# A fused two-block network on one core: two modulation groups summed by VectorE behind attention, one moved into routing, and scatter weights turned by transposes

## The chip, the cores and the metric
One core of a Trainium2 chip runs the whole program in one launch. The metric is the device time of one execution in microseconds; lower is better.

## The reference, cut to what matters
The model has 256 tokens of width 1024 and a context of as many rows. The first block is attention (dilated and sliding-window), a norm, and 32 experts of which each token takes 4. The second block has two layers; each begins with a modulation that depends only on two vectors, c (for the tokens, "latent") and c_ctx (for the context):

```python
sc, sc_ctx = jax.nn.silu(c), jax.nn.silu(c_ctx)
for i in range(DEPTH_2):                       # 2 layers
    last = i == DEPTH_2 - 1
    m  = (sc @ w_mod[i] + b_mod[i]).reshape(bsz, 6, d)
    mc = (sc_ctx @ w_mod[i] + b_mod[i]).reshape(6, d)
    sh1, s1, g1, sh2, s2, g2 = [m[:, j, None, :] for j in range(6)]
    sh1c, s1c, g1c, sh2c, s2c, g2c = [mc[j] for j in range(6)]
    h_lat = x * (1.0 + s1) + sh1
    ...
    if not last:
        ctx = layer_norm_2(DN_ALPHA * ctx + g1c * mix_ctx, ...)
```

w_mod is 2 x 1024 x 6144 floats, 48 MB. In the last layer the context's rows are used for shift 1 and scale 1 alone.

## The kernel before, in words
**Weights.** All large weights go through a ring of six slots in SBUF (class Ring, L135). A chunk is 128 x 4096 floats, 2048 KB. `program` (L3633) writes the list of chunks `front`; chunk n takes slot n mod 6. SP issues the loads in that order on one queue, and waits before each until the slot's last chunk has been given back (`chunk_used`). The list: eleven chunks w_in0 to 10, w_mod chunks put between them by the table MODS_BEHIND, w_proj_a, w_proj_b (2), w_out (2), the last four w_mod chunks, then six per expert (moe0.0 to moe31.5), and eight chunks for the context stream among the experts'. From expert 26 on the ring has five slots.

**Modulation** (class Modulation, L271) comes in 6 groups of 2048 columns, each of 4 chunks ("quarters"): groups 0 to 2 are layer 0, groups 3 to 5 layer 1 (3 is shift 1 and scale 1). There are two ways to compute a group. Either VectorE multiplies each half chunk by a column of silu(c) and adds it to a sum of 128 x 2048, one sum for each stream (`add`, L311), so 16 passes a group, and TensorE adds the sum's partitions up with 8 products (`reduce`, L330); or TensorE multiplies the chunks directly (`quarters`, L343), 32 products. Both begin with four products for the biases (`biased`, L295). ACT copies the result out of PSUM (`scalar`), POOL stores it to DRAM (`store`).

**Attention** (function `attention`, L392) has one instruction stream per engine. TensorE makes q, k and v, then 24 units (8 dilated, 16 sliding-window). In a unit TensorE turns the probabilities, makes the scores of the unit after next and then a "piece" of other work that fills the wait for ACT's copy; then the output products. The pieces are the 8 gate tiles in thirds (4, 8 and 4 products) and, before the change, two halves of group 3 (units 4 and 5). Groups 0 to 2 are summed by VectorE before the units. Group 4 is done by TensorE directly behind the units, ahead of the projections. Then TensorE makes eight tiles m0 to m7 of the projections, which VectorE merges with the gates (L830, `merged_ready`), and, after all eight, the four products x0 to x3 with w_out (tile 0 left and right, tile 1 left and right). VectorE adds each to the residual and normalises a tile after its second half.

SP loads up to the chunk behind w_out (`ring.load(sp, ring.at["w_out"] + 3)`, L472), waits for the eighth merge, loads rows, router weights and ctx, goes on with the ring to moe0.1, waits for the norm (`y_ready`), loads the experts' biases, four more chunks, and waits for the biases to land (`loaded`) before it ends its block. All engines end a block together.

**Routing** (class Router, L1285) turns the normed tiles, makes logits, chooses four experts per token, and TensorE has the quarters of group 5 between these steps.

**Experts** (function `moe`, L1410; `expert`). Per expert TensorE makes 4 products for biases, four chunks (16 records each), gathers rows for an expert to come (L1522), turns h with four transposes (L1591), scatters the last expert's result (L1536), turns the scatter weights by two products with the identity (L1598), does a part of the context stream's work where there is one, and two more chunks. A chunk's slot is given back when its products are done. Behind the experts come two stages with gathers of table rows (L1884, L3103) and a linear attention.

## Time and profile before
| | us |
|---|---|
| median of 3 runs | 3541.35 (3540.29 to 3546.61) |
| profiled execution, its own time | 3540.89 |
| its span | 3539.0 |
| PE busy | 3196.0 (90%) |
| DVE busy | 1861.4 (53%) |
| ACT busy | 1112.9 (31%) |
| POOL busy | 877.7 (25%) |
| HBM read | 1366.60 MB, 386 GB/s over the span |

PE is TensorE's products, DVE is VectorE, ACT is ScalarE, POOL GpSimd, SP the engine that issues the loads. Times in the trace count from the span's start. Attention and routing reach 338.7 us, the experts to 1338. A float32 product has two records in PE's counts, a transpose one. The share of an engine over the whole span says little here, since the stages have different limits.

### The profile page before, as it was taken

Reading aid. Unit: us, or ns where it says so; the run is one execution under the profiler, and the core shown is the slowest. Engines: PE = TensorE matmul, PEld = TensorE weight load, DVE = VectorE, ACT = ScalarE, POOL = GpSimd, SP = SyncE. Lnnn points to the kernel's source line nnn. Section 1 sums busy time; section 2 is a strip of 40 time slices with the busy share of each in tenths; the row PEclk is TensorE's granted clock in tenths of the full one; section 3 lists DMA queues with packets and bytes.
Section 4 is the critical chain, followed back from the end, with each engine's and each line's share of the span. In section 5 each row is a group of like instructions: output and inputs, shape, how many; then the busy total and the mean of one; then the engine's idle time right before and its main releaser. Section 6 shows DMA issues by size and latency. Waiting matters only on the chain. (4 is left out here: it accounts for less than half of the span.)

```text
span 3539.0 us, 34401 instructions
## 1 busy us (share of the span) xinstructions
PE 3196.0 (90%) x11192; PEld 1424.6 (40%) x11192; DVE 1861.4 (53%) x4137; ACT 1112.9 (31%) x2999; POOL 877.7 (25%) x796
## 2 busy tenths in 40 slices
PE   8999999999999997989899879998888988877776
PEld 7565343434334433443344323343334444422222
DVE  7743112111221127676776777668764487667664
ACT  1241111110110114444444544445333124434333
POOL 0000000000000003444444444445440024444442
PEclk9999999999999999999999999999999999999999
DMA  9737999999999999999999999999997169999998
GB/s 406 323 144 296 426 427 426 422 419 425 410 428 428 399 427 394 413 421 421 414 416 417 419 421 411 407 421 411 421 403 296 68 278 402 421 421 416 411 419 333
DMA packets 155585, 1370.05 MB, mean 387 GB/s; under 512 B 18335, under 2 KB 18847, under 8 KB 23950
## 3 DMA queue, kind: packets, MB, share of 16 engines
q0 software_dynamic: 111360, 805.46, 55.2%
q1 hardware_dynamic: 44046, 562.36, 38.0%
q8 instruction: 94, 1.54, 0.2%
q14 instruction: 85, 0.70, 0.0%
HBM read 1366.60 MB, written 1.15 MB: 386 GB/s over the span
## 5 line engine op out<-in xcount | busy, mean ns | idle before, releaser
L3103 PE MATMUL ps<-sb_arena,sb_diag 128*128 128x512 f32 x3072 | 1487.6, 623 | 285.6 <-ACT sb_diag L3078 284.5
L1884 POOL DMA_INDIRECT sb_arena<-in_uv,sb_idx x768 | 865.0, 1126 | 2302.1 <-PE ps L3103 1067.2
L3033 DVE SCALAR_TENSOR_TENSOR sb_arena<-sb_arena,sb_H 128x1024 f32<-128x1024 f32 x768 | 941.2, 1226 | 583.6 <-DMA sb_arena<-in_uv,sb_idx 389.0
L3103 PEld LDWEIGHTS ps<-sb_arena,sb_diag 128*128 128x128 f32 x3072 | 562.1, 195 | 1161.4 <-ACT sb_diag L3078 610.1
L1545 PE MATMUL ps<-sb_ring,sb_arena 128*64 128x512 f32 x3072 | 674.4, 594 | 3.6 <-DMA sb_ring<-in_moe 3.6
L3069 ACT ACTIVATE sb_act<-sb_dots 128x1 f32<-128x1 f32 x768 | 154.8, 202 | 1023.3 <-DVE sb_arena L3033 1019.6
L1545 PEld LDWEIGHTS ps<-sb_ring,sb_arena 128*64 128x64 f32 x3072 | 214.3, 137 | 441.7 <-issue 430.0
L1746 DVE TENSOR_SCALAR sb_arena<-ps 128x512 f32<-128x512 f32 x32 | 22.1, 692 | 593.0 <-PE ps L1545 577.4
L3078 ACT ACTIVATE sb_diag<-sb_consts,sb_act 128x128 f32<-128x128 f32 x768 | 308.5, 402 | 28.6 <-PE ps L3103 3.5
L3073 ACT ACTIVATE sb_act<-sb_act,sb_wts 128x1 f32<-128x1 f32 x768 | 226.2, 295 | 25.1
L183 PE MATMUL ps<-sb_ring,sb_arena 128*128 128x512 f32 x416 | 182.0, 594 | 1.9 <-DVE sb_arena L832 1.3
L183 PEld LDWEIGHTS ps<-sb_ring,sb_arena 128*128 128x128 f32 x416 | 77.9, 190 | 97.9 <-issue 96.1
L1753 DVE TENSOR_SCALAR sb_arena<-ps 128x512 f32<-128x512 f32 x32 | 22.1, 692 | 155.1 <-PE ps L1545 155.1
L1662 ACT ACTIVATE sb_arena<-sb_arena 128x512 f32<-128x512 f32 x32 | 20.2, 630 | 249.6 <-DVE sb_arena L1746 249.6
L183 PE MATMUL ps<-sb_ring 128*128 128x128 f32 (+2 forms) x448 | 88.9, 354 | 6.4 <-ACTq L3455 2.9
L388 POOL DMA_DIRECT2D mod_rows<-sb_arena x24 | 12.5, 527 | 329.7 <-ACTq L374 329.7
L1656 ACT ACTIVATE sb_arena<-ps 128x512 f32<-128x512 f32 x32 | 19.1, 597 | 229.3 <-PE ps L1522 229.3
L1679 ACT ACTIVATE sb_arena<-ps 128x512 f32<-128x512 f32 x32 | 19.1, 597 | 227.5 <-PE ps L1545 227.5
L2341 PE MATMUL ps<-sb_ring 128*128 128x512 f32 x192 | 86.4, 593 | 0.0
L183 PEld LDWEIGHTS ps<-sb_ring 128*128 128x128 f32 x448 | 67.9, 194 | 34.8 <-issue 27.5
L183 PE MATMUL ps<-sb_arena,sb_ring 128*128 128x256 f32 x352 | 76.9, 379 | 0.7 <-PE ps L351 0.4
L183 PEld LDWEIGHTS ps<-sb_arena,sb_ring 128*128 128x128 f32 x352 | 66.5, 190 | 10.9 <-issue 2.0
(364 smaller groups left out, 2504.4 us busy)
## 6 DMA issues: line engine op xcount, KB each, us to landing
sb_ring<-in_moe SPq DMA_DIRECT2D x192, 2048.0 KB, 16.4
sb_ring<-in_w_mod SPq DMA_DIRECT2D x24, 2048.0 KB, 14.5
sb_ring<-in_w_in SPq DMA_DIRECT2D x10, 2048.0 KB, 15.7
sb_ring<-in_a_w_in SPq DMA_DIRECT2D x8, 2048.0 KB, 13.6
sb_ring<-in_b_w_in SPq DMA_DIRECT2D x8, 2048.0 KB, 13.0
sb_ring<-in_w_q SPq DMA_DIRECT2D x6, 2048.0 KB, 13.3
sb_arena<-in_uv,sb_idx POOLq DMA_INDIRECT x768, 14.8
sb_ring<-in_a_w_out SPq DMA_DIRECT2D x4, 2048.0 KB, 12.8
```

What stands on the lines that cost most here:

```text
L183: last = nc.tensor.matmul(out, lhs, rhs, start=i == 0, stop=i == len(pairs) - 1)
L1545: last = nc.tensor.matmul(m.ps[n * SLOTS:(n + 1) * SLOTS, bank, :], lhs(k + KT // 2 * (c % 2), n), w[:, k, n * 512:(n + 1) * 512], start=f ...
L1662: nc.scalar.activation(x.sig, x.g, ACT.Sigmoid, scale=SW_ALPHA).then_inc(M(name("sig_ready", p)), 1)
L1746: nc.vector.tensor_scalar(x.g, m.ps[:, 4, :], LIMIT, None, ALU.min).then_inc(M(name("g_ready", p)), 1)
L1753: nc.vector.tensor_scalar(x.u, m.ps[:, 5, :], LIMIT, -LIMIT, ALU.min, ALU.max).then_inc(M(name("u_ready", p)), 1)
L1884: pool.indirect_dma_start(row_buffer(m, n), None, d[f"uv{layer}"], bass.IndirectOffsetOnAxis(m.idx[:, pair % 2, k:k + 1], 0))\
L2341: last = nc.tensor.matmul(m.ps[:, where[0], :], lhs(k), w[:, k, :], start=k == 0, stop=k == KT - 1)
L3033: nc.vector.scalar_tensor_tensor(out=u, in0=u, scalar=1.0, in1=m.H[:, order[i], :], op0=ALU.mult, op1=ALU.mult, accum_out=m.dots[:, n_ % P ...
L3069: nc.scalar.activation(a, m.dots[:, n_ % PK:n_ % PK + 1], ACT.Gelu_apprx_tanh).then_inc(M("gelu_done"), 1)
L3073: nc.scalar.activation(a, a, ACT.Copy, scale=m.wts[:, pair % 2, k:k + 1]).then_inc(M("act_ready"), 1)
L3078: nc.scalar.activation(m.diag[n_ % DIAGS], m.const("ident"), ACT.Copy, scale=a).then_inc(M("diag_ready"), 1)
L3103: last = nc.tensor.matmul(out[h], m.diag[n_ % DIAGS], uv[b][:, D + h * 512:D + (h + 1) * 512], start=opens, stop=ends)
```

## The change
1. Group 3 leaves the pieces of attention: the pieces are the 24 thirds of the gates alone, two ahead of the units, so the last two units have none. Group 3 is now computed by TensorE in routing, where group 5 was, and its chunks are loaded last, ahead of the experts'.
2. Group 4 leaves TensorE. VectorE sums it behind attention, for the latent stream only (8 passes): three quarters ahead of the first merge, the fourth ahead of the merge of m3. TensorE's `reduce` has 4 selecting products instead of 8 and stands behind m7.
3. Group 5 is summed by VectorE likewise: a quarter ahead of the merge of m5, one each ahead of x0, x1 and x2. TensorE's `reduce` of it stands ahead of x3.
4. With one sum, each pass waits for the pass before it; with two sums it waited for the last but one.
5. The table of loads: w_in7 to w_in10 follow w_in6 and its chunks directly, then w_mod16 to 19, w_proj_a, w_proj_b, w_out, w_mod20 to 23, w_mod12 to 15.
6. Per expert, the scatter weights are turned by `nc.tensor.transpose` in place of a product with the identity.

```diff
-LATE_MODS = 1
-SUMMED_MODS = 3
-MOD_FILL, MOD_END = 3, 4
-MODS_BEHIND = (1, 3, 4, 6, 8, 9, 12, 16, 16, 16, 20)
+MOD_ORDER = (0, 1, 2, 4, 5, 3)
+FIRST_MODS = 3
+LATE_MOD = MOD_ORDER[-1]
+MODS_BEHIND = (1, 3, 4, 6, 8, 9, 12)
...
+        self.sums = {0: gates, 1: tokens, 2: gates, 4: [m.part(0, 2048)], 5: [m.part(2048, 2048)]}
...
         for k in range(2):
-            for stream in range(2):
-                out, scale = self.sums[i % 2][stream], self.silu_c[:, 2 * quarter + k, stream:stream + 1]
-                if self.adds >= 2:
-                    dve.wait_ge(M("mod_add"), self.adds - 1)
+            for stream, out in enumerate(self.sums[i]):
+                scale, behind = self.silu_c[:, 2 * quarter + k, stream:stream + 1], len(self.sums[i])
+                if self.adds >= behind:
+                    dve.wait_ge(M("mod_add"), self.adds - behind + 1)
...
         self.biased(pe, i)
-        pe.wait_ge(self.M("mod_summed"), i + 1)
+        pe.wait_ge(self.M("mod_summed"), MOD_ORDER.index(i) + 1)
...
-    pieces = [("gate", n, third) for n in range(8) for third in range(3)]
-    pieces[6:6] = [("mod", MOD_FILL, half) for half in range(2)]
-    ahead = len(pieces) - len(units)
+    pieces = [(n, third) for n in range(8) for third in range(3)]
+    ahead = 2
     gm = banks.plan([("m", i) for i in range(KT)], [0, 1, 2, 3])
+    mod.plan([4, 5], [0, 1])
...
-                piece(*pieces[ahead + u])
+                if ahead + u < len(pieces):
+                    piece(*pieces[ahead + u])
...
-            mod.tensor(pe, MOD_END)
...
+            mod.reduce(pe, 4)
             pe.wait_ge(M("merged_ready"), KT)
             for i in range(4):
+                if i == 3:
+                    mod.reduce(pe, 5)
                 t, half = i // 2, i % 2
...
+            for quarter in range(3):
+                mod.add(dve, 4, quarter)
             for i in range(KT):
                 where = gm["m", i]
+                if i == 3:
+                    mod.add(dve, 4, 3)
+                if i == 5:
+                    mod.add(dve, 5, 0)
...
             for i in range(4):
+                if i < 3:
+                    mod.add(dve, 5, 1 + i)
                 t, half = i // 2, i % 2
...
-                    last = nc.tensor.matmul(m.ps[:, 4, t * P:(t + 1) * P], x.weigh[:, t, :], m.const("ident"), start=True, stop=True)
+                    last = nc.tensor.transpose(m.ps[:, 4, t * P:(t + 1) * P], x.weigh[:, t, :], m.const("ident"))
...
-            end = MODS_BEHIND[n]
-            front += [(f"w_mod{u}", d["w_mod"][u], SLOT) for u in range(sent, end)]
-            sent = end
+            if n < len(MODS_BEHIND):
+                front += [mod_chunk(u) for u in range(sent, MODS_BEHIND[n])]
+                sent = MODS_BEHIND[n]
+        front += [mod_chunk(u) for u in range(16, 20)]
         front += [("w_proj_a", d["w_proj_a"], 2 * D)]
         front += [("w_proj_b", d["w_proj_b"][n], SLOT) for n in range(2)]
         front += [("w_out", d["w_out"][n], SLOT) for n in range(2)]
-        front += [(f"w_mod{u}", d["w_mod"][u], SLOT) for u in range(4 * (N_MOD - LATE_MODS), 4 * N_MOD)]
+        front += [mod_chunk(u) for u in (*range(20, 24), *range(12, 16))]
```

SP's order from the load of ctx to the second chunk of the experts; ctx, the router's weights and the two rows of L907 (L912 now) stand behind SP's wait for the eighth merge, and `chunk_usedN` is the giving back of slot N. Before:

```order
L1297 DMA sb_X<-in_ctx 128x2x1024
L152 DMA sb_ring<-in_w_mod 128x4096 [waits chunk_used1]
L152 DMA sb_ring<-in_w_mod 128x4096 [waits chunk_used2]
L152 DMA sb_ring<-in_w_mod 128x4096 [waits chunk_used3]
L152 DMA sb_ring<-in_moe 128x4096 [waits chunk_used4]
L152 DMA sb_ring<-in_moe 128x4096 [waits chunk_used5]
```

And now:

```order
L1302 DMA sb_X<-in_ctx 128x2x1024
L152 DMA sb_ring<-in_w_mod 128x4096 [waits chunk_used3]
L152 DMA sb_ring<-in_w_mod 128x4096 [waits chunk_used4]
L152 DMA sb_ring<-in_w_mod 128x4096 [waits chunk_used5]
L152 DMA sb_ring<-in_w_mod 128x4096 [waits chunk_used0]
L152 DMA sb_ring<-in_w_mod 128x4096 [waits chunk_used1]
L152 DMA sb_ring<-in_w_mod 128x4096 [waits chunk_used2]
L152 DMA sb_ring<-in_w_mod 128x4096 [waits chunk_used3]
L152 DMA sb_ring<-in_moe 128x4096 [waits chunk_used4]
L152 DMA sb_ring<-in_moe 128x4096 [waits chunk_used5]
```

Four w_mod chunks more (w_mod12 to 15) stand between the wait for the merges and the experts' first chunk.

TensorE's order from x1 to the first turned tile (L183 are w_out's products, L1316 and L1321 the transposes of y). Before:

```order
L183 MATMUL ps<-sb_ring,sb_arena 128x512 [waits bank_free5,chunk_in5]
L183 MATMUL ps<-sb_ring,sb_arena 128x512 x7
L183 MATMUL ps<-sb_ring,sb_arena 128x512 [waits bank_free6,chunk_in4]
L183 MATMUL ps<-sb_ring,sb_arena 128x512 x7
L183 MATMUL ps<-sb_ring,sb_arena 128x512 [waits bank_full6,bank_free7,chunk_in5]
L183 MATMUL ps<-sb_ring,sb_arena 128x512 x7
L1316 MATMUL ps<-sb_consts,sb_X 128x128 [waits bank_full7,y_ready,bank_free4]
L1316 MATMUL ps<-sb_consts,sb_X 128x128 x3
L1316 MATMUL ps<-sb_consts,sb_X 128x128 [waits y_ready,bank_free5]
```

And now, from x1 on, where L304 are the bias products and L342 the selecting products of group 5:

```order
L183 MATMUL ps<-sb_ring,sb_arena 128x512 [waits bank_free5,chunk_in1]
L183 MATMUL ps<-sb_ring,sb_arena 128x512 x7
L183 MATMUL ps<-sb_ring,sb_arena 128x512 [waits bank_free6,chunk_in0]
L183 MATMUL ps<-sb_ring,sb_arena 128x512 x7
L304 MATMUL ps<-sb_arena,sb_consts 2x512 [waits bank_full6,bank_free1]
L304 MATMUL ps<-sb_arena,sb_consts 2x512 x3
L342 MATMUL ps<-sb_arena,sb_consts 2x512 [waits mod_summed]
L342 MATMUL ps<-sb_arena,sb_consts 2x512 x3
L183 MATMUL ps<-sb_ring,sb_arena 128x512 [waits bank_free7,chunk_in1]
L183 MATMUL ps<-sb_ring,sb_arena 128x512 x7
L1321 MATMUL ps<-sb_consts,sb_X 128x128 [waits bank_full7,y_ready,bank_free4]
L1321 MATMUL ps<-sb_consts,sb_X 128x128 x3
```

The reduction of group 5 stands between x2 and x3 and waits for VectorE's sum.

VectorE's order now, behind the eighth merge (L325 are summing passes of group 5, L846 and L848 a residual and its statistics):

```order
L325 SCALAR_TENSOR_TENSOR sb_arena<-sb_ring,sb_wts,sb_arena 128x2048 [waits chunk_in3,rows_in,mod_add,x_in,merged_ready]
L325 SCALAR_TENSOR_TENSOR sb_arena<-sb_ring,sb_wts,sb_arena 128x2048 [waits mod_add]
L846 SCALAR_TENSOR_TENSOR sb_X<-sb_X,ps 128x512 [waits mod_add,bank_full4]
L848 BN_STATS sb_stats<-sb_X 128x6 [waits bank_free4]
L325 SCALAR_TENSOR_TENSOR sb_arena<-sb_ring,sb_wts,sb_arena 128x2048 [waits mod_add,chunk_in4,dve_step]
L325 SCALAR_TENSOR_TENSOR sb_arena<-sb_ring,sb_wts,sb_arena 128x2048 [waits mod_add]
L846 SCALAR_TENSOR_TENSOR sb_X<-sb_X,ps 128x512 [waits mod_add,bank_full5]
L848 BN_STATS sb_stats<-sb_X 128x6 [waits bank_free5]
```

and behind the norm of tile 0

```order
L325 SCALAR_TENSOR_TENSOR sb_arena<-sb_ring,sb_wts,sb_arena 128x2048 [waits mod_add,chunk_in5,y_ready]
L325 SCALAR_TENSOR_TENSOR sb_arena<-sb_ring,sb_wts,sb_arena 128x2048 [waits mod_add]
L846 SCALAR_TENSOR_TENSOR sb_X<-sb_X,ps 128x512 [waits mod_add,bank_full6]
```

Before, no summing pass stood in this place: now x0 waits behind the quarter in w_mod21 (`chunk_in3`), x1 behind w_mod22 and x2 behind w_mod23.

## Rows read from the trace of the kernel before

**Rows 1.** Windows by stage: attention's units, the experts. us, busy us (count) by engine, PEclk, DMA share, GB/s
```profile
155.00:247.40 92.40, 89.19 (x560) 61.20 (x564) 49.05 (x166) 34.95 (x101) 2.04 (x4) 1.00 0.37 147
...
338.70:1338.00 999.30, 989.49 (x4816) 406.61 (x4816) 176.55 (x410) 132.45 (x219) 5.88 (x8) 1.00 1.00 421
```

**Rows 2.** Timeline of PE in attention: start, us, engine, line, operation, count
```profile
158.47 3.62 PE L351 MATMUL ps<-sb_ring,sb_wts 128*2 128x512 f32 x32
...
239.85 3.62 PE L543 MATMUL ps<-sb_H,sb_ring 128*128 128x256 f32 x16
...
244.49 1.89 PE L543 MATMUL ps<-sb_H,sb_ring 128*128 128x256 f32 x8
...
247.28 1.03 PE L302 MATMUL ps<-sb_arena,sb_consts 24*2 24x512 f32 x8
```

**Rows 3.** Timeline of PE: projections and w_out's products
```profile
255.73 17.50 PE L183 MATMUL ps<-sb_arena,sb_ring 128*128 128x256 f32 x80 [0.44 <-PE ps L351]
...
292.38 20.87 PE L183 MATMUL ps<-sb_ring,sb_arena 128*128 128x512 f32 x48 [1.34 <-DVE sb_arena L832]
...
313.56 7.10 PE L183 MATMUL ps<-sb_ring,sb_arena 128*128 128x512 f32 x16 [0.30 <-PE ps L183]
```

**Rows 4.** Timeline of SP, DMAs issued from attention's end to the experts
```profile
246.50 4.03 SPq L152 DMA_DIRECT2D sb_ring<-in_w_proj_b  x2
...
294.43 1.75 SPq L152 DMA_DIRECT2D sb_ring<-in_w_mod  x3
...
313.38 7.74 SPq L152 DMA_DIRECT2D sb_ring<-in_moe  x2
...
325.74 0.33 SPq L1302 DMA_DIRECT2D sb_arena<-in_b_gate  x1
...
327.25 10.06 SPq L152 DMA_DIRECT2D sb_ring<-in_moe  x4
```

**Rows 5.** Issue to landing: w_proj_b 246.5, w_mod 294.4-295.7, b_down, moe 327.2-337.0
```profile
DMA to landing us min/median/max: 8.7/9.3/9.9
...
DMA to landing us min/median/max: 11.3/15.7/19.8
...
DMA to landing us min/median/max: 4.0/4.0/4.0
...
DMA to landing us min/median/max: 8.3/11.9/14.8
```

**Rows 6.** Timeline of DVE: four summing passes, x1 and the norm of tile 0
```profile
39.81 9.14 DVE L323 SCALAR_TENSOR_TENSOR sb_arena<-sb_ring,sb_wts,sb_arena 128x2048 f32<-128x2048 f32 x4 [0.22 <-DVE sb_arena L323]
...
306.49 0.69 DVE L841 SCALAR_TENSOR_TENSOR sb_X<-sb_X,ps 128x512 f32<-128x512 f32 x1 [5.42 <-PE ps L183]
...
309.90 1.54 DVE L892 SCALAR_TENSOR_TENSOR sb_X<-sb_X,sb_stats,sb_H 128x512 f32<-128x512 f32 x2
```

**Rows 7.** Experts 3 and 31: PE's timeline and moe chunks issued 412.6 to 416.1
```profile
429.86 14.03 PE L1545 MATMUL ps<-sb_ring,sb_arena 128*64 128x512 f32 x64
...
L152 SPq DMA_DIRECT2D sb_ring<-in_moe x2: 327/328/328, 412.6 to 416.1; - x2
...
DMA to landing us min/median/max: 22.6/23.4/24.1
...
445.70 0.60 PE L1591 MATMUL ps<-sb_consts,sb_arena 128*128 128x128 f32 x4
...
1321.50 3.65 PE L1545 MATMUL ps<-sb_ring,sb_arena 128*64 128x512 f32 x16 [1.24 <-DMA sb_ring<-in_moe]
...
1329.26 0.71 PE L1598 MATMUL ps<-sb_consts,sb_arena 128*128 128x128 f32 x4
```

**Rows 8.** Windows of the experts in which the stream stood still
```profile
715.00:740.00 25.00, 25.00 (x102) 8.67 (x102) 1.90 (x4) 4.99 (x6) 0.00 (x0) 1.00 0.95 393
...
900.00:920.00 20.00, 20.00 (x63) 7.73 (x61) 2.13 (x6) 0.00 (x0) 0.00 (x0) 1.00 0.87 353
...
1140.00:1165.00 25.00, 25.00 (x127) 17.40 (x125) 2.22 (x7) 2.67 (x5) 0.00 (x0) 1.00 0.80 326
```

More of the change, by code:

```diff
@@ L363, in scalar @@
         banks.wait_full(act, where)
-        if i >= 2:
-            act.wait_ge(M(f"mod_out{i % 2}"), 64 * (i // 2))
+        nth = MOD_ORDER.index(i)
+        if nth >= 2:
+            act.wait_ge(M(f"mod_out{nth % 2}"), 64 * (nth // 2))
         for g in range(4):
@@ L447, in _ @@
         def _(pool):
-            for i in range(early):
+            for i in MOD_ORDER[:-1]:
                 mod.store(pool, i)
-            mod.stored(pool, early)
+            mod.stored(pool, N_MOD - 1)
         @block.sync
@@ L528, in _, with piece @@
             banks.fill(channel_tile(w, 0, m.ps[:, where[0], 0:T]), where)
-            def piece(kind, n, third):
-                if kind == "mod":
-                    if third == 0:
-                        mod.biased(pe, n)
-                    mod.quarters(pe, n, range(2 * third, 2 * third + 2))
-                    return
+            def piece(n, third):
                 name, where = f"w_in{7 + n // 2}", gg["gate", n]
@@ L733, in _ @@
                 turn(u)
-                kind, n, third = pieces[ahead + u]
-                if kind == "mod" and third == 1:
-                    mod.scalar(act, n)
-                if kind == "gate" and third == 2:
-                    gates_out(n)
+                if (ahead + u) % 3 == 2 and ahead + u < len(pieces):
+                    gates_out((ahead + u) // 3)
             for i in range(4):
@@ L1452, in _ @@
         def _(pool):
-            for i in range(N_MOD - LATE_MODS, N_MOD):
-                mod.store(pool, i)
+            mod.store(pool, LATE_MOD)
             pool.wait_ge(M("idx_ready"), 1)
@@ L1498, in down_biases @@
                 pe.wait_ge(M("late_gatesT"), 1)
-                for i in range(N_MOD - LATE_MODS, N_MOD):
-                    pe.wait_ge(M(f"bank_free{mod.where[i][0]}"), mod.where[i][1] + 1)
+                pe.wait_ge(M(f"bank_free{mod.where[LATE_MOD][0]}"), mod.where[LATE_MOD][1] + 1)
                 for i in range(4):
@@ L1645, in _ @@
         def _(act):
-            for i in range(N_MOD - LATE_MODS, N_MOD):
-                mod.scalar(act, i, "late_staged")
+            mod.scalar(act, LATE_MOD, "late_staged")
             count = largest(act)
@@ L3638, in program, with mod_chunk @@
         banks = Banks(M)
+        def mod_chunk(u):
+            return f"w_mod{u}", d["w_mod"][u], SLOT
         front, sent = [], 0
```

48 lines of the change are left out of this document (24 added, 24 removed).

## The prediction
> **What bounds the kernel now.** I read the windows by stage first. In each [rows 1] the reader is to compare PE's busy time with the DMA share. In attention PE is busy 89.2 of 92.4 us and DMA has a share of 0.37: PE bounds that stretch. In the expert stage (338.7 to 1338) both are full: PE 989.5 of 999.3 us, DMA share 1.00 at 421 GB/s. A weight chunk is 2048 KB, 2.097 MB. Three w_mod chunks issued between 294.4 and 295.7 landed at 294.4+11.3 = 305.7 and at the last 295.7+19.8 = 315.5 [rows 4, 5], 4.9 us each, or 428 GB/s, and I take that as the full rate. An expert needs six, 29.4 us, and the stage has 31.2 us per expert, with 8 chunks for the context stream besides. Which one ends last? The PE rows answer [rows 7]: for expert 3 the fourth chunk lands at 416.1+24.1 = 440.2 and PE is through with all four at 429.86+14.0 = 443.9, later by 3.7, its own time for one chunk; for expert 31 PE waits 1.24 us for a landing. So **the weight stream sets the end of the stage**. It stood still itself only where PE held the ring, at experts 12, 18 and 26 [rows 8]: (1-393/428)x25 = 2.0, (1-353/428)x20 = 3.5 and (1-326/428)x25 = 6.0 us. Whatever delays the stream ahead of the experts delays the kernel, and a faster PE only buys back those standstills.
>
> **Part 1, groups 3 and 4 leave PE.** In attention group 3 is 1.0 us of bias products, as the row of group 4 has them, and twice 3.6 us [rows 2], 8.3 us in all. The gate pieces move up two units. The last two units lose their pieces of 3.62 and 1.89 us [rows 2] and then wait for ACT's copy of the turned probabilities; I take 4.3 us for the pair instead of 7.9 (from the transposes 0.5 us ahead of 239.85 to 247.28): two times transposes, ACT's copy and output products, about 2.2 us each. That is 3.6 us, and the units before gain 3.1 (8.3 gone, 5.5 moved in, 0.3 of waits gone). Attention ends 6.7 us earlier, at 240.7. Group 4 behind it, from 247.28 to 255.73 [rows 2, 3], goes too, so the projection could start at 241.2. It can't: w_proj_b's first chunk takes the slot of w_in10, which is free only after the last gate piece, which now lies in the third unit from the end, 0.8 us ahead of the pair's start at 236.4, at 235.6; before, it was issued at 246.5 and took 8.7 us [rows 4, 5] under group 4's cover. Now it lands at about 243.9. PE starts at 243.9 instead of 255.73: **-11.8 us**.
>
> **Part 2, the adds behind attention.** A pass over 128x2048 takes 2.26 us start to start with two sums in turn [rows 6]; with one sum each pass waits for the one before it, and dependent operations stand 0.04 us apart where the norm shows it (306.49+0.69 to 307.22 is the next), so 2.39, or 2.57 if the 0.22 of a chunk's end comes each time. A quarter is 2 passes, 4.96 us (bounds 4.7 and 5.2); a group's first is 3.9. Three quarters of group 4 run from 241.3 to 255.1 while PE makes m0 to m2. VectorE catches up, and the last merge stays 1.3 us behind PE, at 280.6 (292.33-11.7). The chunks of w_proj_b and w_out wait for VectorE's slots now, but have 10 us or more. PE's reduction of group 4 costs 1.0 + 1.0 us (half the selecting products) where it idled 1.34: w_out's products start at 281.3, not 292.38. Nothing is lost so far: -11.0 us.
>
> **Part 3, group 5 among w_out's products.** Here I expect the stall. SP still loads only up to w_mod20 before it waits for the last merge, then rows and ctx, then w_mod21 to 23. The first landed at 294.4+11.3 = 305.7, 13.4 us after the merge [rows 4, 5]; now at 294.0. VectorE's order is add, x0, add, x1 with the norm of tile 0, add. That is 294.0 + 4.96 + 1.45 + 4.96 + 5.0 (x1 and the norm, 306.49 to 311.44 [rows 6]) + 4.96 = 315.3. PE has x2 at 281.3+21.2 = 302.5, issues the biases and **waits for the sum from 303.5 to 315.3**, with x3 queued behind: x3 ends at 315.3+1.1+7.1 = 323.5. Before it ended 320.7 (313.56+7.1) [rows 3]. The 11 us are gone and 2.8 us more.
>
> **Part 4, the stream.** This is the larger half. w_mod12 to 15, four chunks or 19.6 us of stream, were loaded in attention, where DMA is idle at 0.37. Now they stand behind w_mod23 and ahead of the first expert's chunks. w_mod13 takes the slot of w_out's second half, free when x3 is done: issued at 323.8, after a standstill of some 13 us (w_mod12, with x2's slot, lands at 310.5). From a queue at rest a chunk took 8.3 to 8.7 us, half a microsecond of it other traffic [rows 5]; I take 7.8: landed at 331.6, w_mod15 at 341.4. Its counterpart w_mod23 landed at 295.7+19.8 = 315.5: the chunk ahead of moe0.0 is 25.9 us late. From there the first six expert chunks took until 337.0+14.8 = 351.8 [rows 4, 5], 36.3 us for 29.4 of transfer and 0.9 of biases, the rest, 6.0, standstill, since each waited for a slot; those now queue at once. With 0.2 us of the same kind behind it, the stream is **19.7 us late** when it reaches expert 3. PE is late by less at first: the last quarter of group 3 waits for w_mod15, and SP's bias loads, issued at 328.6 behind moe0.1 in its queue, land at about 352 (before: 4.0 us after their issue [rows 4, 5]). SP ends its block only then, and every engine with it, so the experts start at about 353 for 338.7, 14.5 us late. At expert 3 PE meets the stream and is 19.7 us late as well.
>
> A rule weighed here: in these windows the stream runs at 421 to 428 GB/s. The Trainium skill (DMA: Bandwidth & Descriptors, Where 436 GB/s comes from) says that for loads from HBM the HBM side binds at about 358 GB/s. The trace doesn't agree; by that figure four chunks would be 23.4 us, an estimate from the page, and the sum 3.8 us more.
>
> **Part 5, the turned weights.** Per expert the two products against the identity are a row of 0.71 us, the four transposes of h just ahead 0.60 [rows 7]: two of them 0.30, less overlap. I take 0.35 us off PE per expert (bounds 0 and 0.45). It only counts where PE holds the stream: from expert 3 to the standstill at expert 18, 15 x 0.35 = 5.3 us, 19.7 - 5.3 = 14.4 (the stream alone would be at 19.7 - 5.5 = 14.2 with the standstills of experts 12 and 18 gone, so PE decides, barely). At 23 both meet again; to the standstill of expert 26 another 3 x 0.35 = 1.1: **+13.3 us at the end of the experts**. What follows is the same program, shifted.
>
> By another rule the term is larger: the Trainium skill (TensorE: Matmul & The Clock Gate, Terms) gives FP32 a transpose mode that is 4x faster. The trace's own transposes are 2.4x faster per piece (0.15 for 0.36 us). By 4x the row of 0.71 would be 0.18 and the saving some 0.48 us, an estimate from the page, and the sum 18 x 0.13 = 2.3 us less.
>
> **Sum.** -11.8 + 0.8 (reduce 4) + 13.8 (reduce 5 and the wait, x3 at +2.8), then the four chunks: +25.9 at the last of them, -6.2, -5.3, -1.1 = **+13.3**. The profiled execution took 3540.89 us around a span of 3539.0, 0.46 under the median 3541.35, to which I add: **3554.6 us**. Two measurements of this kernel can be told apart from about 0.2%, 7 us.
>
> **Rivals.** (a) *Group 5's wait isn't there* (VectorE done by 303.5). Then x3 ends near 311.5, w_mod15 lands at 329.3, 13.8 late; -6.2 gives 7.6, -5.3 and -1.1 give +1.3: 3542.6. For it: only that PE sits still in no such place before. Against: the landing 13.4 us after the merge. 0.09. (b) *Faster*: PE, not the stream, paces the experts. Then they would start with group 3's end, about 343.2 for 337.8 (+5.4), if also the biases don't wait in the queue, and 32 x 0.35 = 11.2 us come back: -5.8, or 3535.5; with (a) on top more. It decides if the stream can run ahead of 428 GB/s. Against: no slack between landing and release at expert 3, and the waits at expert 31. 0.05. (c) *The turned weights cost what they did*: the transposing form brings nothing, 6.4 us stay: 3561. Against: the h transposes. 0.08. (d) *Slots come later than I think* (dependent passes of 2.57 us, 8.7 us from issue to landing, the biases' barrier costing a further standstill): 3 to 6 us more, 3559. 0.13. My forecast, 3549 to 3558: 0.65.
>
> **Numbers.** The range 3546 to 3562 holds forecast, (c) and (d), and leaves out (a) and (b). Slower by over 0.2% (above 3548.4): forecast, (c), (d), 0.85 less something for slack in any of my terms, 0.82; within: (a) and part of (b), 0.12; faster 0.06.
>
> **What would show it.** PE in the w_out products: reducing products of group 5 with about 12 us idle before them, released by VectorE. DMA at rest for over 10 us between 310 and 324. First gather of the experts near 353, first release of a slot near 364. Standstills at experts 12 and 18 gone or halved, the last chunk landing about 13 us later than 1331. The row of the turned weights at about 0.35 us. Wrong would be: no idle before that reduction, or a first gather before 345.

## The result and the profile after

The changed kernel takes 3562.58 us (median of five runs, 3558.74 to 3567.90) against 3543.03 for the kernel before: ratio 1.0056, 95% interval 1.0042 to 1.0071. That is **19.6 us slower**; the prediction said 13.3 slower, and a range that ended at 3562. A second set of five runs of the same program gave 3561.81, ratio 1.0061 (1.0048 to 1.0074). The profiled execution took 3567.9 us around a span of 3565.7, the slowest of the five; the profiled one of the second set took 3558.53, the fastest of its five. Differences between single executions are therefore good for the mechanism, and medians for the sum.

The windows by stage, with the columns of [rows 1]:

```profile
155.00:240.00 85.00, 80.88 (x480) 58.93 (x478) 48.88 (x164) 33.18 (x95) 0.00 (x0) 1.00 0.21 77
338.70:360.70 22.00, 7.97 (x61) 3.50 (x60) 3.22 (x20) 1.09 (x3) 0.00 (x0) 0.67 1.01 397
360.70:1362.00 1001.30, 989.68 (x4752) 401.29 (x4752) 176.53 (x410) 132.47 (x219) 5.88 (x8) 0.99 1.00 422
```
Attention ends at 239.5 instead of 247.35, 7.9 us earlier, and DMA rests even more in it (share 0.21). The experts take nearly as long as before, 1001.3 us at 422 GB/s for 999.3 at 421. What is new lies between: the middle row, 22 us, in which DMA is full (1.01) and PE busy for 8.

PE's timeline behind attention, to set against [rows 3]:

```profile
242.85 19.19 PE L183 MATMUL ps<-sb_arena,sb_ring 128*128 128x256 f32 x80 [3.36 <-DMA sb_ring<-in_w_proj_b]
...
280.15 1.03 PE L304 MATMUL ps<-sb_arena,sb_consts 24*2 24x512 f32 x8 [0.30 <-PE ps L183]
...
316.54 1.89 PE L342 MATMUL ps<-sb_arena,sb_consts 128*2 128x512 f32 x8 [12.39 <-DVEq L331]
318.35 9.10 PE L183 MATMUL ps<-sb_ring,sb_arena 128*128 128x512 f32 x16
...
332.08 3.16 PE L354 MATMUL ps<-sb_ring,sb_wts 128*2 128x512 f32 x16
...
360.78 3.78 PE L1525 MATMUL ps<-sb_arena,sb_X 128*128 128x128 f32 x16 [12.17 <-DVE sb_arena L1715]
365.24 3.78 PE L1525 MATMUL ps<-sb_arena,sb_X 128*128 128x128 f32 x16 [0.69 <-ACT sb_arena L1658]
```
The first row is the start of the projections, at 242.85 for 255.73; behind a wait of 3.36 us m0 to m3 took 19.19 us where they took 17.50. The third row is the predicted wait: PE stood 12.39 us for VectorE's sum of group 5, and x3 began at 318.35 and took 9.10 us where it took 7.10. The experts' first two gathers take 3.78 us each.

VectorE at the same place, the last rows of its work on group 5, with the columns of [rows 6]:

```profile
295.37 4.74 DVE L325 SCALAR_TENSOR_TENSOR sb_arena<-sb_ring,sb_wts,sb_arena 128x2048 f32<-128x2048 f32 x2 [14.24 <-DMA sb_ring<-in_w_mod]
...
301.72 4.74 DVE L325 SCALAR_TENSOR_TENSOR sb_arena<-sb_ring,sb_wts,sb_arena 128x2048 f32<-128x2048 f32 x2
...
311.58 4.74 DVE L325 SCALAR_TENSOR_TENSOR sb_arena<-sb_ring,sb_wts,sb_arena 128x2048 f32<-128x2048 f32 x2
```
The first add waits for w_mod21's landing; the last ends at 316.3. In between VectorE is never idle for more than 0.15 us: three quarters at 4.74 us, with x0, x1 and a norm among them, set the end of PE's wait.

SyncE's timeline, then the loads of w_mod13 to moe0.1, of the biases, and of moe0.2 to 0.5, from issue to landing, to set against [rows 4, 5]:

```profile
283.24 45.62 SPq L152 DMA_DIRECT2D sb_ring<-in_w_mod  x7
328.90 1.16 SPq L152 DMA_DIRECT2D sb_ring<-in_moe  x2
332.54 0.33 SPq L1307 DMA_DIRECT2D sb_arena<-in_b_gate  x1
...
335.28 12.89 SPq L152 DMA_DIRECT2D sb_ring<-in_moe  x4
```

```profile
L152 SPq DMA_DIRECT2D sb_ring<-in_w_mod x3: 328/430/432, 327.6 to 328.4; - x3
...
DMA to landing us min/median/max: 7.7/16.7/28.0
```

```profile
DMA to landing us min/median/max: 26.1/26.1/26.1
```

```profile
DMA to landing us min/median/max: 28.8/30.8/31.3
```
SP was held from 303.1 to 327.6 at w_mod13 (inside the first row); w_mod15, the third of that group, lands 16.7 us behind its issue at 328.4, at 345.1. The biases, 4.0 us from issue to landing before, now take 26.1. SyncE's list of waits in that stretch gives the other end of the same thing:

```profile
SPq L445 <- DMA sb_arena<-in_b_down: 11.2, 1, 11.2
```
And the three windows of [rows 8], 24 us later:

```profile
739.00:764.00 25.00, 25.00 (x97) 9.05 (x97) 0.00 (x0) 4.36 (x5) 0.00 (x0) 1.00 0.99 413
924.00:944.00 20.00, 20.00 (x64) 8.19 (x64) 2.13 (x6) 0.38 (x1) 0.00 (x0) 1.00 0.93 381
1164.00:1189.00 25.00, 25.00 (x126) 17.26 (x124) 2.22 (x7) 2.66 (x5) 0.00 (x0) 1.00 0.82 334
```
Counted off the GB/s as in the prediction, 0.9 us of standstill is left at expert 12 ((1-413/428)x25), 2.2 of 3.5 at 18, 5.5 of 6.0 at 26. Counted off the DMA share in the same rows, the rest of the DMA went from 1.3, 2.6 and 5.0 us to 0.3, 1.4 and 4.5. By either count the one at 18 is about halved, not gone.

### The profile page after: what moved, and what is told of

It is laid out like the page before. It is cut to its first block and busy times, and to the rows that moved or that the text cites. A ratio compares the mean times of both kernels' runs of the same rounds, so it can differ in the third digit from the quotient of the medians.

```text
span 3565.7 us, 34079 instructions
## 1 busy us (share of the span) xinstructions
PE 3194.6 (90%) x11016; PEld 1420.9 (40%) x11016; DVE 1896.9 (53%) x4153; ACT 1114.1 (31%) x2999; POOL 857.8 (24%) x796
## 5 line engine op out<-in xcount | busy, mean ns | idle before, releaser
L1886 POOL DMA_INDIRECT sb_arena<-in_uv,sb_idx x768 | 845.1, 1100 | 2326.7 <-PE ps L3105 1092.1
L183 PE MATMUL ps<-sb_ring,sb_arena 128*128 128x512 f32 x416 | 184.0, 599 | 0.3 <-PE ps L183 0.3
L183 PEld LDWEIGHTS ps<-sb_ring,sb_arena 128*128 128x128 f32 x416 | 78.7, 192 | 98.8 <-issue 98.8
L325 DVE SCALAR_TENSOR_TENSOR sb_arena<-sb_ring,sb_wts,sb_arena 128x2048 f32<-128x2048 f32 x42 | 97.0, 2349 | 20.1 <-DMA sb_ring<-in_w_mod 18.3
L183 PE MATMUL ps<-sb_ring 128*128 128x128 f32 (+2 forms) x448 | 88.9, 354 | 6.4 <-ACTq L3457 2.9
L183 PEld LDWEIGHTS ps<-sb_ring 128*128 128x128 f32 x448 | 68.0, 195 | 35.3 <-issue 28.0
L183 PE MATMUL ps<-sb_arena,sb_ring 128*128 128x256 f32 x352 | 78.6, 385 | 3.7 <-DMA sb_ring<-in_w_proj_b 3.4
## 6 DMA issues: line engine op xcount, KB each, us to landing
sb_ring<-in_w_q SPq DMA_DIRECT2D x6, 2048.0 KB, 12.6
```

The source lines that it names most:

```text
L183: last = nc.tensor.matmul(out, lhs, rhs, start=i == 0, stop=i == len(pairs) - 1)
L325: ins = nc.vector.scalar_tensor_tensor(out=out, in0=w[:, k, :], scalar=scale, in1=out, op0=ALU.mult, op1=ALU.add)
L1886: pool.indirect_dma_start(row_buffer(m, n), None, d[f"uv{layer}"], bass.IndirectOffsetOnAxis(m.idx[:, pair % 2, k:k + 1], 0))\
```

## Experiments

Each was timed beside the kernel before on one chip; medians of 5 to 12 runs; the kernel before itself came out at 3541.5 to 3542.9 there. "m0.5" and the like is the landing of that expert chunk in the profiled execution.

### The transposing form by itself

```diff
-  last = nc.tensor.matmul(m.ps[:, 4, t * P:(t + 1) * P], x.weigh[:, t, :], m.const("ident"), start=True, stop=True)
+  last = nc.tensor.transpose(m.ps[:, 4, t * P:(t + 1) * P], x.weigh[:, t, :], m.const("ident"))
```
In the kernel before:

> The kernel before with one edit, the scatter weights turned by the transposing form. Theory of the prediction: 0.35 us per expert leave TensorE, and count only where TensorE holds the weight stream, up to the standstills at experts 12, 18 and 26 (2.0, then 6 x 0.35 = 2.1, then 8 x 0.35 = 2.8): about 7 us less, 3535.5 us for 3542.5. Rival, TensorE paces every expert: 32 x 0.35 = 11.2 us less, 3531.3. Rival, the form brings nothing: 3542.5.

Measured 3537.36 us, ratio 0.9989 (0.9980 to 0.9997), 4.5 us less. The reverse, in the changed kernel:

> The changed kernel with the matmul form put back for the scatter weights. If the transposing form buys back standstills as predicted, this is 6 us slower than the changed kernel, 3569; if TensorE paces every expert, 11 us slower, 3574; if the form brings nothing, 3562.6. Standstills at experts 12 and 18 would be back at about 2 and 3.5 us.

Measured 3568.85 us, ratio 1.0071 (1.0059 to 1.0084), 6.3 and 7.0 us above the two medians of the changed kernel. TensorE's groups by line and shape from 430 to 1330 us, the turned weights' row in the kernel before and in the first of the two:

```profile
L1598 PE MATMUL ps<-sb_consts,sb_arena 128*128 128x128 f32 x116 | 20.6, 300 | 0.0
```

```profile
L1598 PE MATMUL ps<-sb_consts,sb_arena 128*128 128x128 f32 x58 | 12.7, 301 | 0.0
```
Half the records, each of the same 0.30 us, and 7.9 us of busy time over 29 experts: 0.27 us per expert, not 0.35. The part that counts is as predicted, only what falls up to the standstills: the last chunk lands at 1307.4+19.2 = 1326.6 us instead of 1331.2, 4.6 earlier, not 7. The Trainium skill's transpose mode (TensorE: Matmul & The Clock Gate, Terms), 4x by the page, isn't seen in these rows: a pair of turned tiles costs 0.44 us for 0.71, in half the records.

### The wait for group 5's sum

```diff
             for i in range(4):
-                if i == 3:
-                    mod.reduce(pe, 5)
                 t, half = i // 2, i % 2
...
                     ring.done(pe, "w_out", half)
+            mod.reduce(pe, 5)
             router.turn(pe, 0)
```


> The changed kernel with the reduction of group 5 moved behind the last w_out product, the adds left where they are. Theory: TensorE's wait for the sum holds x3, and with it the slot of w_out's second half, which w_mod13 takes. Then x3 ends near 311.5 us instead of 327.5, w_mod15 lands near 329.5 instead of 345.1, the experts start near 343 instead of 360, and the whole is some 15 us faster, 3547.5. Rival, the four chunks alone delay the stream and the wait was beside them: 0 to 3 us, 3560 to 3562.6. Rival, the wait only moves, to the norms behind VectorE: x3 early, but the experts start no earlier than 355: 3558.

Measured 3546.78 us, ratio 1.0012 (1.0004 to 1.0021): **15.8 us faster** than the changed kernel's 3562.58. Its timelines of PE and of SyncE:

```profile
305.46 7.10 PE L183 MATMUL ps<-sb_ring,sb_arena 128*128 128x512 f32 x16 [0.30 <-PE ps L183]
...
318.81 1.89 PE L342 MATMUL ps<-sb_arena,sb_consts 128*2 128x512 f32 x8 [5.05 <-DVEq L331]
```

```profile
305.28 8.69 SPq L152 DMA_DIRECT2D sb_ring<-in_w_mod  x4
314.01 4.99 SPq L152 DMA_DIRECT2D sb_ring<-in_moe  x2
```
x3 ends at 312.6. PE still waits, 5.05 us, but with w_out's slots given back: all six loads up to moe0.1 are issued by 319, five of them by 314. w_mod15 landed at 331.5, m0.5 at 364.2 (378.8 in the changed kernel). The theory's numbers hold to 2 us, but for the experts' start, at 346.1 for 343. Of these 15.8 us the sum on VectorE is not itself the cost: the place of the wait, ahead of the product that holds a slot, is.

### The biases' barrier

```diff
-            ring.load(sp, ring.at["moe0.0"] + 2)
+            ring.load(sp, ring.at["w_mod12"] + 2)
             sp.wait_ge(M("y_ready"), 2 * TT)
             router.rest(sp)
```


> The changed kernel with the wait for the norms and the three small bias loads moved in SyncE's program from behind moe0.1 to behind w_mod13. Theory: the bias loads land near 337 us, ahead of four chunks in the queue, the block ends with the last quarter of group 3 near 349 instead of 360, and the standstills of moe1.0, 1.4 and 1.5 (3.0 + 1.3 + 1.3 = 5.6 us over 4.9 each) go: 3557. Rival, the stream is held by its own landings and the late start costs nothing at the end: 3562.6, with the experts starting early all the same. Rival, the wait for the norms holds back w_mod14 by more than it gives: slower than 3563.

Measured 3562.35 us, ratio 1.0056 (1.0043 to 1.0069): no difference, the first rival. The biases' time to landing and PE's first gather:

```profile
DMA to landing us min/median/max: 4.0/4.0/4.0
```

```profile
353.11 2.05 PE L1525 MATMUL ps<-sb_arena,sb_X 128*128 128x128 f32 x16 [1.22 <-DVE sb_arena L1715]
```
The experts start 7.7 us earlier and it brings nothing measurable: m1.5 lands at 410.1 here, at 410.4 in the second profile of the unedited kernel (the last run below). The stream, not the experts' start, is the later there. The 2.8 us over 4.9 at moe1.0, which the expectation called a standstill, are still there (7.7): moe1.0 was issued at 363.7, 13.6 us before the chunk ahead of it landed, so the queue wasn't empty; what lies between is two loads of 512 KB for the context, landing at 378.1 and 379.9.

### TensorE's clock behind its waits

```diff
             pe.wait_ge(M("o_ready"), len(units))
+            products(nc, m.ps[:, 3, :], [(ident, m.consts[:, 0:512])] * 3)
...
         self.biased(pe, i)
+        if i == 5:
+            products(nc, m.ps[:, 2, :], [(m.const("ident"), m.consts[:, 0:512])] * 12)
         pe.wait_ge(self.M("mod_summed"), MOD_ORDER.index(i) + 1)
...
             router.turn_gates(pe)
+            products(nc, m.ps[:, 5, :], [(ident, m.consts[:, 0:512])] * 12)
```


> The changed kernel with products of constants that nothing reads, put on TensorE ahead of three of its waits: 3 ahead of the projection's wait for w_proj_b, 12 ahead of the wait for group 5's sum, 12 behind the last step of the routing. Theory: the waits leave TensorE's granted clock low for the work behind them (x3 took 9.10 us for 7.10, group 3's first quarter 3.16 for 1.90, the experts' first gathers 3.78 for 2.05 each); with the engine kept at work those rows are back at their short times, w_mod13 is issued some 2 us earlier, and the first expert's releases come some 10 us after the first gather instead of 18: the whole is 4 to 8 us faster, 3557. Rival, the clock's cost is hidden beside the stream: 3562. Rival, the fillers outlast their waits and delay what follows: above 3563.

Measured 3555.00 us, ratio 1.0038 (1.0025 to 1.0051): **7.6 and 6.8 us faster** than the changed kernel's two medians, with 27 products more. The windows of the changed kernel and of this one:

```profile
303.00:330.00 27.00, 14.11 (x50) 5.11 (x50) 16.49 (x19) 3.90 (x8) 2.05 (x4) 0.68 0.30 96
345.00:360.00 15.00, 3.15 (x18) 0.45 (x18) 0.02 (x1) 0.08 (x1) 0.00 (x0) 0.54 1.01 382
360.00:375.00 15.00, 12.80 (x48) 8.31 (x50) 2.21 (x12) 4.75 (x7) 2.04 (x4) 0.50 1.01 428
```

```profile
303.00:330.00 27.00, 24.67 (x102) 11.10 (x101) 18.84 (x31) 5.56 (x10) 2.04 (x4) 1.00 0.39 150
345.00:360.00 15.00, 13.45 (x50) 6.40 (x42) 1.48 (x8) 2.35 (x4) 0.00 (x0) 0.97 1.02 384
360.00:375.00 15.00, 13.18 (x73) 5.52 (x73) 2.64 (x8) 3.11 (x4) 2.04 (x4) 1.00 1.00 415
```
and PE's timeline in this one:

```profile
302.51 10.57 PE L183 MATMUL ps<-sb_consts 128*128 128x512 f32 x24
...
315.98 7.13 PE L183 MATMUL ps<-sb_ring,sb_arena 128*128 128x512 f32 x16
...
358.20 2.05 PE L1529 MATMUL ps<-sb_arena,sb_X 128*128 128x128 f32 x16 [1.19 <-DVE sb_arena L1719]
```
The granted clock is 0.68, 0.54 and 0.50 in the first (0.50 is the 1.2 GHz level, the others are stretches with both levels), and 1.00, 0.97 and 1.00 with the fillers, nearly all 2.4 GHz. x3 is back at 7.13 us and ends at 323.1, where the prediction had it (323.5), the gathers at 2.05. w_mod15 lands at 342.0 and m1.5 at 406.6, which is 2.9 and 3.8 us ahead of the second profile of the unedited kernel. The last expert chunk is issued at 1328.9 for 1332.9 in that profile and 1336.3 in the first: by the traces the clock costs 4.0 to 7.4 us up to there, by the medians 6.8 to 7.6 in all.

### The four chunks by themselves

```diff
+        front += [(f"again{u}", d["w_mod"][u], SLOT) for u in range(12, 16)]
...
             mod.quarters(pe, early, [3])
+            for u in range(12, 16):
+                ring.wait(pe, f"again{u}")
+                ring.done(pe, f"again{u}")
```
In the kernel before with the transposing form, so 3537.4 us is what it adds to; `done` gives a slot back:

> The kernel before with the transposing form (3537.4) and four chunks more in the stream, w_mod12 to 15 loaded a second time behind w_mod23; nothing computes with them, TensorE waits for each behind group 5 and gives its slot back. This is the price of four chunks by itself. Theory: moe0.5 lands near 369 instead of 352, the experts start near 353, and the time is some 17 us more, 3554 (at most 19.6 + 4.5 for the standstills that the later stream no longer finds: 3557 at most, 3551 at least). Rival, the stream had slack ahead of the experts: 3542.

Measured 3566.99 us, ratio 1.0069 (1.0055 to 1.0082), 29.6 us more: outside what was expected. The profile splits it. From expert 2 to expert 24 every chunk is issued 20 to 21.5 us later than without the four (the fourth of expert 4 at 484.7 for 463.4): 19.6 of transfer and nothing given back. Then, 20 us apart, the same work without and with the four:

```profile
1130.00:1160.00 30.00, 30.00 (x148) 18.84 (x146) 4.12 (x11) 3.29 (x6) 0.00 (x0) 1.00 0.85 352
```

```profile
1150.00:1180.00 30.00, 30.00 (x150) 18.92 (x148) 4.12 (x11) 3.29 (x6) 0.00 (x0) 1.00 0.52 212
```
At expert 26 the ring goes from six slots to five. moe26.0 takes slot 1 in both kernels, but with four chunks more in the list that slot was last held by the context's last chunk and not by moe25.2: moe26.0 is issued 29.5 us behind moe25.5 where it was 6.9, and at the end of the experts the lateness is 31.2 us where it was 21.3. That is this experiment's own doing, since the changed kernel has as many chunks as the one before. The 21.3 are what the four chunks cost in the stream up to expert 24.

### Groups 4 and 5 on VectorE without the four chunks

```diff
-MOD_ORDER = (0, 1, 2, 4, 5, 3)
-MODS_BEHIND = (1, 3, 4, 6, 8, 9, 12)
+MOD_ORDER = (0, 1, 2, 3, 4, 5)
+MODS_BEHIND = (1, 3, 4, 6, 8, 9, 12, 16)
...
+    pieces[6:6] = [("mod", 3, half) for half in range(2)]
...
-            mod.quarters(pe, LATE_MOD, [0])
```
with the reduction of group 5 late, as above.

> The changed kernel with the reduction of group 5 behind the last w_out product, and group 3 back in attention with its four chunks, loads in the order of the kernel before: groups 4 and 5 stay on VectorE, and no modulation chunk stands between w_mod23 and the first expert's. Theory: the four chunks in the stream are what the change costs. Attention and projection then run as before (projection from about 255), w_mod23 lands near 315.5, moe0.5 near 352.5, and the time is that of the kernel before with the transposing form alone, 3537 to 3540. Rival, the sums on VectorE cost by themselves (norms late behind the adds, experts starting after 350): 3548 or more.

Measured 3549.10 us, ratio 1.0017 (1.0009 to 1.0026): the expectation missed, and the rival is right. The timelines of DVE and PE, and SyncE's waits:

```profile
322.57 4.74 DVE L324 SCALAR_TENSOR_TENSOR sb_arena<-sb_ring,sb_wts,sb_arena 128x2048 f32<-128x2048 f32 x2
...
333.92 1.54 DVE L896 SCALAR_TENSOR_TENSOR sb_X<-sb_X,sb_stats,sb_H 128x512 f32<-128x512 f32 x2
```

```profile
347.87 3.78 PE L1522 MATMUL ps<-sb_arena,sb_X 128*128 128x128 f32 x16 [1.22 <-DVE sb_arena L1711]
```

```profile
SPq L1306 <- DVE sb_X L896: 14.5, 1, 14.5
```
The last add stands ahead of x2's residual, so the norms end at 335.5; the biases, issued as soon as they do, go out at 335.5 where [rows 4] has 325.7. SyncE waits 14.5 us for them with moe0.2 to 0.5 behind it, and moe0.2 lands 11.5 us over its 4.9. Another 4.1 us go at moe1.4 and 1.5, which land 7.4 and 6.5 us behind the chunk ahead of them, with the experts starting at 347.9. So the version without the four chunks is no faster than the one with them and the same late reduction (3546.78): in that one the stream still has the four chunks to move while SyncE waits for the norms. The two prices lie beside each other and don't add up.

> The run without the four chunks in the stream (groups 4 and 5 on VectorE, group 3 back in attention) came out at 3549, not 3538; its ring stood still 11.5 us at moe0.2, while SyncE waited for the norms, which stood behind VectorE's last add. Here that last add is moved behind both norms, and the reduction of group 5 behind the logits of the second tile. Theory: the norms end near 330 us instead of 335.5, moe0.2 lands some 5 us earlier, and the time is 3544. Rival, it was TensorE's start of the experts, not the norms: 3549. Rival, the last slot released later gives it back: 3549 or more.

Its edit puts `mod.add(dve, 5, 3)` behind both norms, `mod.reduce(pe, 5)` behind `router.logit_products(pe, 1)` and ScalarE's copy of group 5 (`mod.scalar(act, 5)`) behind the second turned tile. Measured 3561.34 us, ratio 1.0048 (1.0034 to 1.0062): worse by 12, though norms (331.4) and m0.5 (356.3) came as expected. The experts began late:

```profile
360.06 3.78 PE L1524 MATMUL ps<-sb_arena,sb_X 128*128 128x128 f32 x16 [8.71 <-DVE sb_arena L1713]
```
and moe1.0, which needs the slot of moe0.0, stood still for 21.4 us. With GpSimd's wait for the last store taken out (`mod.stored(pool, N_MOD - 1)`):

> The run with the norms ahead of VectorE's last add came out at 3561: its norms ended at 331.4 and moe0.5 landed at 356.3 instead of 361.2, as expected, but the experts started at 360 instead of 348, since the block's end waited on GpSimd for group 5's rows to be stored, and moe1.0 stood still for 21.4 us. Here GpSimd waits only for the first five groups' stores, as the kernel before does. Theory: the experts start near 352.5 us, moe1.0's standstill falls by the same 7.5 us, and the time is 3553 to 3554: ring slots of the first expert tie the stream to the experts' start. Rival, the late start costs nothing since the stream is the bound: 3561, with the experts starting earlier all the same.

Measured 3560.87 us, ratio 1.0053 (1.0039 to 1.0067), and the gather at 359.86: the edit didn't do what it was for. GpSimd issues the store's four transfers from 350.4 to 352.5 and the block ends at 358.9 all the same. What every engine does at the block's end (L444) shows why:

```profile
L444 POOLq DRAIN x1: 6815/6815/6815, 351.9 to 351.9; - x1
```
TensorE and VectorE are through at 352.2. GpSimd's own drain (DRAIN, the instruction that closes its part of the block) takes 6.8 us, to 358.7, 1.0 us past the landing of the last of the four stores (351.95+5.7 = 357.65). With the wait in place the drain took 2.0 us, from 356.9 to 358.9, behind a last landing at 356.6. In these two runs, then, the block doesn't end before the stores have landed, with the wait or without it. Some 5 us of the late start lie elsewhere: VectorE's choice for the second tile sits 5.21 us idle until ScalarE's exponential at 350.2, which stands behind the 2.4 us of the copy of group 5. Whether an earlier start would have brought the 8 us isn't settled.

### A version that beats both

```diff
-MODS_BEHIND = (1, 3, 4, 6, 8, 9, 12, 16, 16, 16, 20)
+MODS_BEHIND = (1, 3, 4, 6, 8, 9, 12, 16, 16, 16, 17)
...
-        front += [("w_proj_a", d["w_proj_a"], 2 * D)]
-        front += [("w_proj_b", d["w_proj_b"][n], SLOT) for n in range(2)]
+        front += [("w_proj_b", d["w_proj_b"][0], SLOT), mod_chunk(17)]
+        front += [("w_proj_a", d["w_proj_a"], 2 * D), ("w_proj_b_", d["w_proj_b"][1], SLOT), mod_chunk(18), mod_chunk(19)]
...
-            mod.tensor(pe, MOD_END)
...
+            mod.reduce(pe, MOD_END)
             pe.wait_ge(M("merged_ready"), KT)
...
             both = m.part(7168, 2, KT, T)
+            for quarter in range(2):
+                mod.add(dve, MOD_END, quarter)
             for i in range(KT):
                 where = gm["m", i]
+                if i in (1, 3):
+                    mod.add(dve, MOD_END, 2 + i // 2)
```
From the kernel before, with `add` and `reduce` of the change and the transposing form.

> A version meant to keep what the change gains and not what it loses. From the kernel before: group 3 stays in attention and group 5 in routing, both on TensorE; group 4 alone goes to VectorE behind attention with one sum; w_proj_b's first half, w_mod17, w_proj_a and w_proj_b's second half are loaded ahead of w_mod18 and 19, so that the projection finds its weights; and the scatter weights are turned by the transposing form. Theory: the projection starts near 247.5 us instead of 255.7, w_out's products near 286 instead of 292.4, the last modulation chunk lands near 309 instead of 315.5, and all of it reaches the end, with the 4.5 us of the transposing form: 3530. Rival, the projection's slots come no earlier, or VectorE's adds hold the merges: 3536 to 3538. Rival, the weight stream ahead of the experts stands still elsewhere and gives the 6 us back: 3537.

Measured **3529.29 us** (3525.80 to 3533.44), ratio 0.9965 (0.9952 to 0.9978), 12.2 us faster than the kernel before. And with the loads in the old order:

> The version of 3529 us with the loads back in the order of the kernel before: group 4 alone on VectorE, the transposing form, nothing else. Theory, from part 1 of the prediction: w_proj_b's first chunk waits for the slot of w_in10, is issued near 245.5 and lands near 253.5 to 254.5, so the projection starts there and not at 247.5; the time is 3537, within 2 us of the transposing form alone. Rival, the gain of the 3529 us version is TensorE's 8.5 us of group 4 whatever the loads: 3530.

Measured 3537.77 us, ratio 0.9991 (0.9982 to 1.0000). The projection's first row in the one and in the other:

```profile
247.03 17.50 PE L183 MATMUL ps<-sb_arena,sb_ring 128*128 128x256 f32 x80 [0.49 <-issue]
...
284.59 20.87 PE L183 MATMUL ps<-sb_ring,sb_arena 128*128 128x512 f32 x48
```

```profile
253.42 18.92 PE L183 MATMUL ps<-sb_arena,sb_ring 128*128 128x256 f32 x80 [7.00 <-DMA sb_ring<-in_w_proj_b]
```
So of group 4's 8.5 us on TensorE 7.0 went into the wait for w_proj_b, as part 1 had it, and 1.4 into slower products behind it (18.92 for 17.50), until the loads were put in the order in which slots come free.

The last run is the changed kernel once more:

> The changed kernel once more, unedited, beside the others on one chip. Expected 3562.6 us; the last expert chunk lands between 1350 and 1356 us, and the standstills of moe1.0, 1.4 and 1.5 show again at 3.0, 1.3 and 1.3 us. If its profile shows them smaller, the 27 us between the two profiled executions were partly those executions' own, and the mechanism must account for some 20 us only.

Measured 3561.81 us. In its profile moe1.4 and 1.5 do not stand still, and moe1.5 lands at 410.4 for 413.7. Its second gather took 2.05 us for 3.78:

```profile
360.30 3.78 PE L1525 MATMUL ps<-sb_arena,sb_X 128*128 128x128 f32 x16 [11.41 <-DVE sb_arena L1715]
364.76 2.05 PE L1525 MATMUL ps<-sb_arena,sb_X 128*128 128x128 f32 x16 [0.69 <-ACT sb_arena L1658]
```

```profile
360.00:375.00 15.00, 13.28 (x70) 7.79 (x72) 1.72 (x10) 4.26 (x7) 2.05 (x4) 0.84 1.00 424
```
The granted clock in 360 to 375 us is 0.84 here and was 0.50 in the first profile. The last expert chunk is issued 23.9 us later than in the kernel before in the first profile and 20.5 us later in this one, so 3.4 of the 27 us between the first two profiled executions lie in the first experts of that execution, beside its lower clock. The rest of what sets the two profiles apart lies behind the experts: from the issue of the last expert chunk to the end the 14 profiled executions of all kernels here take 2222.8 to 2229.4 us. The mechanism has to give some 20.

## Why the prediction was right and wrong

**Right: the chain.** Each step of it is in the profile: PE waits for w_proj_b (issued at 234.7, landed at 242.6; predicted 235.6 and 243.9; the first products 242.85), the wait for group 5's sum (12.39 us; 11.8), SP held at w_mod13, four chunks behind each other, the biases behind moe0.1, the standstill at 12 gone but for 0.3 to 0.9 us and the one at 18 about halved. By the experiments: the wait's place costs 15.8 us, the four chunks 21.3 us, the transposing form gives back 4.5 to 7. These are prices of single edits and overlap: with the wait gone the changed kernel still has the four chunks, and is only 9.4 us behind the kernel before with the transposing form, because the front end is some 10 us ahead.

**Wrong: the sizes of three terms, two in part 4 and one in part 5.** The difference of the medians, 19.6 us, lies 6.3 above the sum of 13.3. In the traces the sum is for the last expert chunk, which lands 24.4 us later in the first profile and about 21 in the second (issued 20.5 later). The step that failed first is the price of the work behind the wait: durations from rows at full clock were put behind 12 us of idleness, and the lower clock was put at nothing. The steps on the way, with both profiles:
- *"x3 ends at 323.5", "w_mod15 at 341.4"* was 3.7 us short. The sum came 1.2 us later than worked out (316.54 for 315.3, w_mod21 having landed at 295.2 for 294.0), the reduction took 1.89 for 1.1, and x3 9.10 for 7.10: both durations came from [rows 3], where TensorE had been at work. Behind 12 us of idleness the clock granted is lower. In the second profile w_mod15 landed at 344.8, 3.4 short (reduction 1.88, x3 8.60). The fillers show the clock to be a cause and price it at about 7 us at the end (4.0 to 7.4 by the traces); at w_mod15 it was 2.9 of them, the rest came behind it, where quarters of group 3 and the first gathers pay too. How the 7 divides further isn't settled. The prediction had no such term anywhere, not even in rival (d). In part 2 the same term was mostly hidden by luck: m0 to m3 took 19.19 us for 17.50, and TensorE had started 1.05 us earlier than predicted.
- *"36.3 us for 29.4 of transfer and 0.9 of biases, the rest, 6.0, standstill"* was wrong, and gave back 6.2 us where 2.6 came (2.9 in the second profile). The same stretch before and after, w_mod23 or w_mod15 to moe0.5:

```profile
315.50:351.80 36.30, 32.51 (x219) 16.40 (x219) 11.37 (x48) 9.35 (x15) 2.05 (x4) 1.00 0.94 368
```

```profile
345.10:378.80 33.70, 19.76 (x80) 9.99 (x82) 2.23 (x12) 4.83 (x7) 2.04 (x4) 0.54 1.00 402
```
A share of 0.94 over 36.3 us is 2.2 us of rest. The other 4.7 us are DMA at work below its rate (402 GB/s at a share of 1.00 after): other rows among the chunks. After, 402 GB/s x 33.7 us are 13.5 MB for 12.6 MB of chunks. They were there before and are there now, about the same (4.7 and 4.3 us over the 29.4 of the chunks). The prediction's opening had read the experts' standstills off the GB/s, and part 4 took all that was over the transfer and the bytes of the biases for rest; the share in the same row would have told rest from slow work.
- *"15 x 0.35 = 5.3"* and *"3 x 0.35 = 1.1"* gave back 6.4 us over the experts where 4.4 came (4.5 in the second profile): the form saves 0.27 us per expert, not 0.35, which is 1.4 of the 2.0 over 18 experts. Where the other 0.6 went isn't shown.

In the first profile that is 3.7 + 3.6 + 2.0 us, and 1.7 more between moe0.5 and expert 2, where moe1.4 and 1.5 stood still beside the low clock: 11.0 in all, which with the 13.3 makes 24.3 for the 24.4 measured. In the second it is 3.4 + 3.3 + 1.9, less 0.9 between moe0.5 and expert 2: 7.7, which with the 13.3 makes 21.0. The medians, 6.3 to 7 us above the sum, agree with the second to about 1 us; what follows the experts scatters by more than that.

The prediction's "PE decides, barely" and rival (b) are settled by the two experiments on the form: PE doesn't pace the experts (11 us would have come back). Rival (d) named the biases' barrier (the wait of all engines for their landing) as a price (they landed at 333.4+26.1 = 359.5, not 352, and the experts started at 360.8, not 353); the run with the biases first says it isn't one. The weighed rule of the HBM side at 358 GB/s (the Trainium skill, DMA: Bandwidth & Descriptors, Where 436 GB/s comes from) isn't borne out by this program on one core: 422 GB/s over 1001 us.

Open: whether an earlier start of the experts brings something once the stream is early. Moving the biases' barrier was tried only where the stream was late, and the two runs meant to start the experts behind early norms started them at 360.

## What to carry to other kernels

When work moves from the engine that looks busy to one that looks idle, follow the buffers, not the engines: which transfer's slot does the new waiter hold, and what stands behind that transfer in the queue. In a stage paced by a weight stream a late slot or a chunk put in front of the stream was paid in full down the stream (15.8 us at the end, 21.3 us up to expert 24), a faster engine only up to the next standstill. Prices taken by single edits can lie beside each other: without the four chunks another wait came out, and nothing was won. And before a gap in GB/s is booked as rest to be won back, read the DMA share beside it.
